# Two reorderings in a fused two-block kernel: an activation moved up on ScalarE, a weight split moved down on VectorE

## What is computed

```
def swiglu(h, w_gate, w_up, w_down):
    return (jax.nn.silu(h @ w_gate) * (h @ w_up)) @ w_down
...
# first block, layer 1 (the short convolution, SC)
    p = h @ c_w_in[o]
    gate_b, gate_c, xt = p[..., :W], p[..., W:2 * W], p[..., 2 * W:]
    mix = (gate_b * causal_depthwise_conv(gate_c * xt, c_conv_w[o])) @ c_w_out[o]
...
# second block
    mod = (jax.nn.silu(c) @ ada_w[layer] + ada_b[layer]).reshape(b, N_MOD, D_MODEL)
    mod_ctx = (jax.nn.silu(c_ctx) @ ada_w[layer] + ada_b[layer]).reshape(1, N_MOD, D_MODEL)
...
def context_states(ctx, ...):
    xb, dt_raw = split(modulate(rms_norm_2(ctx, norm_pre), ...) @ w_in[:, ...])
    xb = centred_dwconv_silu(xb, conv_w, conv_b)
    ...
```

## Time and profile before

| | |
|---|---|
| Runs of the kernel before | 1667.98, 1666.6, 1667.0 us |
| Median | 1667.0 us |
| Profiled execution, first to last instruction (span) | 1665.4 us |
| Whole time of the profiled execution | not given beside its span |
| Median less span | 1.6 us |
| PE busy | 1655.6 us, 99% |
| DVE busy | 1229.5 us, 74% |
| ACT busy | 927.8 us, 56% |
| DMA traffic | 359.32 MB, mean 216 GB/s |

### The profile page before, as it was taken

How to read it: one execution, slowest core, us unless ns; L and a number is a source line. 1 busy time by engine, 2 the same in 40 slices (tenths; PEclk the granted TensorE clock), 3 DMA queues, 4 the chain that set the end, 5 groups by cost and what they waited for, 6 DMA issues and landing times.

```text
span 1665.4 us, 22804 instructions
## 1 busy us (share of the span) xinstructions
PE 1655.6 (99%) x8756; PEld 1415.4 (85%) x8756; DVE 1229.5 (74%) x1630; ACT 927.8 (56%) x1396; POOL 148.0 (9%) x210
## 2 busy tenths in 40 slices
PE   9999999999999999999999999999999999999998
PEld 7888888888888888888899888888888889988887
DVE  6888776788888777776688876655766668986564
ACT  6655577655555455545566455554645458655553
POOL 1100100000211001110010011000002012310000
PEclk9999999999999999999999999999999999999999
DMA  8977552787859876687655557554667545357551
GB/s 292 340 261 258 170 191 103 248 295 256 286 174 334 261 247 215 258 301 256 203 166 182 169 174 265 200 189 141 225 213 252 186 144 203 108 180 244 189 190 64
DMA packets 99356, 359.32 MB, mean 216 GB/s; under 512 B 11184, under 2 KB 11440, under 8 KB 99248
## 3 DMA queue, kind: packets, MB, share of 16 engines
q1 hardware_dynamic: 92736, 335.59, 59.0%
q0 software_dynamic: 6368, 22.21, 4.3%
q10 hardware_dynamic: 144, 0.07, 0.0%
HBM read 356.70 MB, written 1.12 MB: 215 GB/s over the span
## 4 chain that ended last, share of the span: by engine, by line
PE 94%; DVE 3%; DMA 2%; issue 1%; ACT 0%; SPq 0%; DVEq 0%; POOLq 0%; POOL 0%; ACTq 0%
PE dn L539 28%; PE gu L494 19%; PE gu L528 10%; PE tp L528 10%; PE gu L527 5%; PE tp L527 5%; PE dn L509 4%; DMA raw<-in_weights 2%; PE gu L524 1%; PE tp L524 1%; PE tp L457 1%; PE dn L528 1%; PE gu L525 1%; PE tp L525 1%; PE dn L494 1%; DVE w_lo L1768 1%
## 5 line engine op out<-in xcount | busy, mean ns | idle before, releaser
L1768 DVE TENSOR_TENSOR w_lo<-raw,w_hi 128x1024 fp32r<-128x1024 f32 x520 | 639.2, 1240 | 217.3 <-ACT w_hi L1135 212.4
L1135 ACT ACTIVATE w_hi<-raw 128x1024 fp32r<-128x1024 f32 x520 | 549.4, 1059 | 322.5 <-PE dn L539 147.7
L494 PE MATMUL gu<-w_hi,hT 128*128 128x512 f32 x1056 | 328.9, 393 | 1.6 <-DVE w_lo L1764 1.1
L528 PE MATMUL gu<-hT,w_hi 128*128 128x512 f32 x728 | 259.6, 396 | 0.0
L528 PE MATMUL tp<-hT,w_hi 128*128 128x512 f32 x728 | 259.5, 396 | 0.0
L539 PE MATMUL dn<-w_hi,actT_hi 128*128 128x512 f32 x608 | 238.8, 393 | 0.0
L539 PE MATMUL dn<-w_lo,actT_hi 128*128 128x512 f32 x608 | 236.9, 390 | 0.0
L539 PE MATMUL dn<-w_hi,actT_lo 128*128 128x512 f32 x608 | 236.7, 389 | 0.0
L494 PEld LDWEIGHTS gu<-w_hi,hT 128*128 128x128 f32 x1056 | 195.6, 188 | 42.6 <-DVE hT L1776 1.5
L494 PE MATMUL gu<-w_lo,hT 128*128 128x512 f32 x528 | 205.9, 390 | 0.0
L527 PE MATMUL gu<-hT,w_lo 128*128 128x256 f32 x728 | 203.1, 279 | 0.0
(11 more groups left out here) (366 smaller groups left out, 2092.3 us busy)
## 6 DMA issues: line engine op xcount, KB each, us to landing
raw<-in_weights SPq DMA_DIRECT2D x563, 512.0 KB, 4.3
arena<-in_ada_w SPq DMA_DIRECT2D x72, 512.0 KB, 4.3
post_row<-in_post_rows POOLq DMA_DIRECT2D x10, 512.0 KB, 5.6
pre_row<-in_pre_rows POOLq DMA_DIRECT2D x10, 512.0 KB, 7.2
mod_row<-mod POOLq DMA_DIRECT2D x9, 512.0 KB, 10.0
shift_row<-mod POOLq DMA_DIRECT2D x5, 512.0 KB, 9.8
x<-in_x_in SPq DMA_DIRECT2D x4, 256.0 KB, 6.0
arena<-in_c_rows POOLq DMA_DIRECT2D x2, 512.0 KB, 9.3
```

The source lines that it names most:

```text
L494: m = pe.matmul(bank, h[:, k, t * P:(t + 1) * P], w[:, r, kk * 512:(kk + 1) * 512], start=k == 0 and q == 0, stop=k == KT - 1 and q == 2)
L528: m = pe.matmul(o, w_hi[:, r, c], hT[:, :, k, :], start=False, stop=k == KT - 1)
L1135: act.activation(o, i, ACT.Copy, **kw).then_inc(done, 1)
L1768: dve.tensor_tensor(w_lo[:, r, :], raw[:, n % RAW, :], w_hi[:, r, :].bitcast(F32), ALU.subtract).then_inc(lo_ready, 1)
```

## The change

Two steps are moved, and nothing is added or taken away.

```
@@ ACT, first_opening @@
                     gate(1, 1)
                     upper(7)
+                    act.wait_ge(c_loaded, 32)
+                    act.activation(c_row[:, :, :], c_row[:, :, :], ACT.Silu).then_inc(c_ready, 1)
                     upper(8)
                     act_upper(0)
@@ ACT, ffn @@
                 after_slots(n0 + 8, 2)
-                if s == 0:
-                    act.wait_ge(c_loaded, 32)
-                    act.activation(c_row[:, :, :], c_row[:, :, :], ACT.Silu).then_inc(c_ready, 1)
                 for j in range(2, STEPS - 1):
@@ DVE, ctx_mix @@
                     if p < 4:
                         after_slots(n0 + 1 + 2 * p, 1)
                         tapped(0, p)
-                        after_slots(n0 + 2 + 2 * p, 1)
+                        if p < 3:
+                            after_slots(n0 + 2 + 2 * p, 1)
                         continue
                     for half in range(2):
                         for t in range(TT):
                             dve.wait_ge(hT_hi_ready, 2 * TT * SC + TT * half + t + 1)
                             in_half_lower(SC, t, half)
+                        if half == 0:
+                            after_slots(n0 + 2 * p, 1)
                     tapped(0, p)
                     after_slots(n0 + 1 + 2 * p, 2)
```

## The result

Over 17 runs each, the changed kernel takes 1669.58 us (1668.03 to 1671.09) against 1667.01 (1666.23 to 1668.3): 2.6 us more, ratio 1.0014, 95% interval [1.0008, 1.0021]. The interval leaves 1 out, so it is slower, by a step that stays under the 0.2% that I had called telling. The forecast was 1668.9 in a range of 1667.0 to 1670.6.

A forecast was written before the change was run, and what follows sets the result against it. PE was taken as the bound, busy 1655.6 of 1665.4 us. Span 1665.4 + 1.4 (Silu) + 0.5 (split) = 1667.3, plus 1.6 from span to median, gave 1668.9 us, range 1667.0 to 1670.6.

The forecast's parts named there:

- ACT waits for the rows, and everything behind it is late: In `ffn_0`, ahead of slot 8: ACT waits until the conditioning rows land at 28.3, making it 4.4 us late.
- What matters is not its 1.90 us but its wait: Silu ahead of slot 8: its wait for the conditioning rows, landing at 28.3, decides, not its 1.90 us.
- PE stands 1.4 us ahead of the first down projection: In `ffn_0`: `actT_lo` ends at 33.1, PE wants it at 31.73, so PE stands 1.4 us.
- Everything that decides this landing is issued earlier, so the change doesn't move it: Conditioning rows' DMAs, issued at 17.1 and 17.9: the later takes 10.4 us, landing at 28.3 as before.
- Part 1: The Silu moved ahead of slot 8's copy in `ffn_0`: costs +1.4 us, with bounds +1.0 and +2.2.
- The transposes of step 2: DVE decides, 1.4 us late: Second step of `ffn_0`: DVE's 7.60 us end at 55.8, PE would arrive at 55.35; transposes 1.4 us late.
- From there on the order is the old one and PE is full: After the second step's transposes in `ffn_0`: order is unchanged and PE full, so the cost stays +1.4 us.
- Slower by more: Rival: ACT's whole 4.4 us passes through the `raw` ring to the second step's transposes; total 1671.9 us; chance 0.06.
- Part 2 costs 0.5 us: Start of `sc`: the 0.59 us stall goes, but DVE loses 0.52 and later transposes slip; +0.5 us, bounds -0.59 and +0.7.
- Early rows: Rival: conditioning rows land before 23.9, the Silu fits ACT's idle time and wins back 0.41 us; total 1667.1; chance 0.05.
- part 2 wins: Rival at the start of `sc`: PE starts 0.59 us earlier and DVE's hole is filled; total 1667.8 us; chance 0.15.
- the early delay is swallowed: Rival: the early 1.4 us ends in a later wait that doesn't move; total 1667.5 us or below; chance 0.07.

The follow-up runs named there:

- e3: Kernel before plus a second, unread Silu of the same size ahead of slot 8's copy, without a wait; the real one stays; 1667.27 us, ratio 1.0001.
- e4: Kernel before with the Silu ahead of slot 8's copy and the rows' DMAs issued early, after the first squares; 1667.12 us, ratio 0.9997.
- e9: Kernel before with the Silu ahead of slot 8's copy and the rows' DMAs issued late, after PE used slot 3; 1669.40 us, ratio 1.0014.
- e1: Kernel before with only the Silu and its wait moved ahead of slot 8's copy, DVE's order unchanged; 1668.63 us, ratio 1.0010.
- e2: Kernel before with only the split of slot n0+16 moved between the low parts, ACT's order unchanged; 1667.94 us, ratio 1.0003.
- e10: Kernel before with the split of slot n0+16 behind all four low parts but ahead of the last taps; 1667.64 us, ratio 1.0005.
- e6: Kernel before with the split of slot n0+16 behind all four low parts and the last pair's taps; 1666.18 us, ratio 0.9998.

## Why the prediction was right, and where it was off

- **ACT waits for the rows, and everything behind it is late.** Right, and shown by e3, e4 and e9. "What matters is not its 1.90 us but its wait" is half of it: the sum itself adds 1.81 us for the Silu, rightly, and without them the stall of 1.4 us would not have come out. The rule "PE starts 4.8 us after the landing" can be read out of my own steps (28.3 to 33.1) and came out as 4.78 three times.
- **PE stands 1.4 us ahead of the first down projection.** The mechanism was right, the size was off: 2.1 us in the profile of the change (10.73 - 8.64), 0.5 in e1, 2.5 in e9. This is the term that was mis-sized. It was built on one landing at 28.3. The change's rows were issued 0.4 us later and the second took 11.1 us instead of 10.4:

```profile
L2546 POOL DMA_DIRECT2D arena<-in_c_rows x2: 562/670/779, 17.5 to 18.3; - x2
DMA to landing us min/median/max: 8.0/9.6/11.1
```

- "Everything that decides this landing is issued earlier, so the change doesn't move it" was true of the order and useless as a number. The landing moves by itself, by more than a microsecond from execution to execution, and so does PE's start (transposes of step 0 at 22.9 to 25.1 us over these profiles). In nine other profiles (all but e1, e4, e9 and the change) the rows are issued at the same point and land 4.3 to 5.4 us behind those transposes; with 4.78 us that would make a stall of 0.4 to 1.6 us, an estimate. So the 5.95 us in the profile of the change is a late case, and my 1.4 lies inside the usual range. Part 1 alone is worth +1.3 us by its median, close to the +1.4.
- **The transposes of step 2: DVE decides, 1.4 us late.** Half right. `actT_lo` came at 48.87, close to my 48.2. But PE was later than I had it, so it found `act_tok` ready and gave back the old stall of 0.41. In e1 and e9 B is 17.44 and 17.92, and there DVE did decide. The 0.64 us at the transposes of step 3, in the profile of the change, I had not foreseen; e1 and e9 don't show it. "From there on the order is the old one and PE is full" failed there: late and slow loads are the path of my rival *Slower by more*, here in small.
- **Part 2 costs 0.5 us: the first stall goes, the train's hole comes back at the taps.** Each step is there: first low part without cover, 0.79 us of hole instead of 0.52; the column slot at once; a wait at block 4; the second transposes right behind the taps. e2's median says +0.57. What failed is the baseline. I set 4.3 to 4.6 us against 4.11. The distance in most profiles is 3.50, so the order costs 0.65 (e2) to 0.84 us (the change) of C against those, and nearly nothing against the profile I read. The end was too high as well, 4.6 against 4.15 and 4.34. The two errors largely cancel, so that the +0.5 comes so near to the +0.57 is luck.
- **Rivals.** Early rows (the case of e4) needed an issue that the change doesn't make. By the Trainium skill, DMA: Bandwidth & Descriptors, section Anatomy of one DMA, a row of 512 KB would take 3.2 us; the rows here show 7.8 (e4) to 11.1 us (the change) for the later of the two. The rule has no term for other transfers under way, and here weight loads are. That part 2 wins, e2 and e10 speak against by C, 4.15 and 4.40 with a floor of 3.50; their times alone don't exclude it. That the early delay is swallowed did not happen: of 2.87 us at 71 us, 3.08 are there at `sc` and 3.31 behind it. The large case of +4.9 did not come.

## What to carry to other kernels

An instruction that waits for a transfer delays all that stands behind it on its engine: before moving one up, add to the landing its own work and the path behind it, and compare that with the time at which the next engine needs the results. The same work ahead of an idle stretch, without the wait, cost nothing here (e3). Work that covers a wait should be swapped only with work that nobody waits for at the end of the same train; here the split fits behind the taps (C 3.50), not between the low parts or ahead of the taps (4.15 to 4.40). A stall of half a microsecond in one profile may be that execution's own, so look at it in a second one before building an edit on it.

## What I had not expected of the hardware

Two stalls of PE that I took for properties of the kernel come and go. At `sc` C is 4.11 or 4.10 us in two profiles, and 3.50 to 3.62 in five others with the same order at that place. In the two, the copy of the weight slot that ACT waits longest for there starts 9.2 us ahead of PE's first six transposes, in the five others 9.6 to 9.9 us. The kernel before and e3:

```profile
877.35 1.06 ACT L1135 ACTIVATE w_hi<-raw 128x1024 fp32r<-128x1024 f32 x1 [5.09 <-DMA raw<-in_weights]
```

```profile
878.29 1.06 ACT L1135 ACTIVATE w_hi<-raw 128x1024 fp32r<-128x1024 f32 x1 [4.39 <-DMA raw<-in_weights]
```

With the transposes at 886.53 and 888.15 that is 9.18 and 9.86 us ahead: a load that lands 0.7 us sooner, and the stall is not there. That this load is the cause is read from the profiles; it was not tried by itself. The other one is B, at 16.78 to 17.92 us. Four kernels have the old order of all engines in `ffn_0`: the kernel before, e2, e6 and e10 show 17.19, 16.81, 17.88 and 16.92 us.
